# Latent attention heads in eight pairs instead of four groups, in a two-block forward pass in float32

## The chip, the cores and the metric

The kernel runs on one core of a Trainium2 chip. The metric is the device time of one execution in microseconds (us), lower is better; the time quoted is the median of several executions.

## The reference

One sequence of 256 tokens, width 1024, goes through a block of two layers and then through a second block with three further attentions and a mixture of experts. The change touches only the attention of the first block's second layer:

```python
def mla_attention(u, q_lora_norm, w_dq, w_uq, w_o, k_nope, k_rope, v, cos, sin):
    cq = rmsnorm(u @ w_dq, q_lora_norm)                  # 256 tokens x 256
    q = jnp.einsum('bsr,rhd->bshd', cq, w_uq)            # 16 heads x (128 + 64)
    q_nope = q[..., :QK_NOPE_DIM]
    q_rope = apply_rope(q[..., QK_NOPE_DIM:], cos[None, :, None], sin[None, :, None])
    ...
        s = (jnp.einsum('bqhd,bkhd->bhqk', qn_b, k_nope)
             + jnp.einsum('bqhr,bkr->bhqk', qr_b, k_rope))   # per block of 128 queries
        s = s.astype(jnp.float32) * scale
        s = jnp.where(mask[None, None], s, -jnp.inf)         # causal
        p = jax.nn.softmax(s, axis=-1).astype(v.dtype)
        return jnp.einsum('bhqk,bkhd->bqhd', p, v)
    ...
    return o @ w_o                                       # (16 * 128) x 1024
```

K and V of the 16 heads are made from one latent of 128 numbers a token: `k_nope = c_kv @ w_uk`, `v = c_kv @ w_uv`; the rotary key is shared by all heads.

## The kernel before

Every weight passes through a ring of three slots. The SyncE queue (SP) loads a block into `RAW`, of at most 128 x 2048 numbers, as soon as `lo_ready` says that the slot is free. ScalarE (ACT) rounds it to fp32r in `WH` and VectorE (DVE) writes the remainder `RAW - WH` to `WL`; both steps are called `prep`. TensorE (PE) then multiplies in three fp32r passes (`product`: high by high, high by low, low by high) and signals `w_used`. Matmuls on plain float32 data (scores, rotation, outputs) are two passes each in the trace. All orders are written out by hand, one instruction stream for each engine, tied by semaphores.

The latent attention has this order. PE makes the compressed query (`dq`), the keys of the 16 heads (`uk`; ACT copies them to `KN`) and the values (`uv`, eight products of 512 columns, alternately in the PSUM banks `GB` and `UB`; DVE copies them to `V`). Then come four groups of four heads. Group `g` has its query weights in three blocks of the ring. PE makes all queries of the group in `ACC`, ACT copies them to `T`, PE multiplies the rotary part by a rotation matrix into `MB`, and DVE makes the rope in three steps (`rope`: times cosine, the rotated times sine, sum). PE writes the scores of the four heads to the four banks of `ACC`, which is why the next group's queries can start only when the scores have been read. In front of the softmax ACT and DVE prepare the next group's three blocks, or in the last group the first three blocks of the output projection `wo` (`latent_parts`, `blocks`). DVE adds the mask into `PR` and takes the maxima (`group_scores`), ACT makes the exponentials and their sums in place (`group_probs`), and DVE scales them; PE turns the probabilities (`turn`), ACT copies them to `PT`, PE multiplies them with `V` (`weigh`), and ACT and DVE store the output as high and low part in `OH` and `OL` (`group_outputs`). PE begins the next group only when the last output of this one has been stored (`at_ol`). After the fourth group the projection takes eight blocks of 24 matmuls (`down`), and the next feed-forward stage follows. The other attentions of the kernel use the same helpers.

## Time and profile before

| | |
|---|---|
| median of three executions | 2256.55 us (2255.88 to 2256.81) |
| profiled execution | 2257.95 us, its span 2256.2 us |
| busy: PE, DVE, ACT | 2004.4, 1381.1, 996.8 us |
| mean granted TensorE clock | 0.945 of 2.4 GHz |
| values, groups and projection | 691.45 to 849.95 us of the span |

Times within the span are in us from its start. A row of the timeline gives the start, the busy time, the engine, the line, the operation with what it writes and reads, and in brackets how long the engine had stood idle and which instruction released it. The granted clock has two levels here, 1.00 (2.4 GHz) and 0.50 (1.2 GHz); a value between is a mean over a stretch. PEld is PE's weight load, which lies beside its matmuls.

### The profile page before, as it was taken

How to read it: one execution, taken by the hardware profiler on the slowest of the kernel's cores; microseconds unless marked ns; L12 is line 12 of the kernel's file. 1: busy time of each engine (PE TensorE's matmuls, PEld its weight loads, DVE VectorE, ACT ScalarE, POOL GpSimd, SP SyncE). 2: the span in 40 equal slices, each digit the busy share in tenths (PEclk: the TensorE clock that was granted, in tenths of full speed). 3: DMA queues.
4: the chain of work that ended last, by engine and by line, in shares of the span. 5: the costliest groups of instructions: out<-in, count | busy, mean ns of one | idle time of the engine just before them, and what ended most of it. 6: DMA issues, size and time to landing. Idle time of an engine off the chain costs nothing.

```text
span 2256.2 us, 24516 instructions
## 1 busy us (share of the span) xinstructions
PE 2004.4 (89%) x9607; PEld 1649.7 (73%) x9607; DVE 1381.1 (61%) x1878; ACT 996.8 (44%) x1270; POOL 70.2 (3%) x94
## 2 busy tenths in 40 slices
PE   6998899979997789998987899886779999999995
PEld 5787688768876567886766678775668888877774
DVE  4776566666764547676346655548654445478885
ACT  4344334444344434434335434413534434367774
POOL 1000000000000000000000010000000000000000
PEclk9999899989999999998888999978889999999998
DMA  8776367647761246774103586401236657599994
GB/s 285 237 240 226 119 233 244 228 141 239 235 208 32 72 155 204 246 236 160 57 24 131 168 291 207 155 19 57 75 141 225 220 177 235 176 335 364 359 358 160
DMA packets 293803, 432.80 MB, mean 192 GB/s; under 512 B 12164, under 2 KB 244935, under 8 KB 293431
## 3 DMA queue, kind: packets, MB, share of 16 engines
q1 hardware_dynamic: 273696, 356.65, 47.6%
q0 software_dynamic: 17792, 66.99, 8.5%
q10 hardware_dynamic: 2198, 7.58, 0.8%
q8 instruction: 76, 1.25, 0.2%
q14 instruction: 41, 0.33, 0.0%
HBM read 422.27 MB, written 14.68 MB: 194 GB/s over the span
## 4 chain that ended last, share of the span: by engine, by line
PE 73%; issue 10%; DVE 10%; ACT 4%; DMA 1%; ACTq 0%; POOLq 0%; POOL 0%; DVEq 0%; SPq 0%
PE acc L1742 8%; PE acc L1744 8%; PE acc L1743 8%; PE gate_bank L1742 7%; PE gate_bank L1743 7%; PE gate_bank L1744 7%; PE up_bank L1742 6%; PE up_bank L1743 6%; PE up_bank L1744 6%; DVE w_low L1083 3%; PE acc L1880 2%; ACT w_high L663 2%; PE turn_bank L1854 1%; DMA raw<-in_e_ffn_up 1%; PE misc_bank L1902 1%
## 5 line engine op out<-in xcount | busy, mean ns | idle before, releaser
L1083 DVE TENSOR_TENSOR w_low<-raw,w_high 128x2048 fp32r<-128x2048 f32 (+5 forms) x388 | 779.4, 2020 | 506.9 <-ACT w_high L663 506.8
L663 ACT CAST w_high<-raw 128x2048 fp32r<-128x2048 f32 (+5 forms) x388 | 651.8, 1692 | 634.8 <-PE acc L1744 306.5
L1742 PE MATMUL acc<-w_high,hidden_high 128*128 128x512 f32 x682 | 275.2, 404 | 16.5 <-DVE hidden_low L1681 9.4
L1743 PE MATMUL acc<-w_low,hidden_high 128*128 128x512 f32 x682 | 269.2, 395 | 0.0
L1744 PE MATMUL acc<-w_high,hidden_low 128*128 128x512 f32 x682 | 268.3, 393 | 0.0
L1742 PE MATMUL gate_bank<-w_high,u_high 128*128 128x512 f32 (+2 forms) x620 | 246.0, 397 | 19.7 <-DVE w_low L1083 8.6
L1743 PE MATMUL gate_bank<-w_low,u_high 128*128 128x512 f32 (+2 forms) x620 | 238.7, 385 | 0.0
L1744 PE MATMUL gate_bank<-w_high,u_low 128*128 128x512 f32 (+2 forms) x620 | 238.7, 385 | 0.0
L1742 PE MATMUL up_bank<-w_high,u_high 128*128 128x512 f32 (+1 forms) x588 | 228.5, 389 | 0.0
L1744 PE MATMUL up_bank<-w_high,u_low 128*128 128x512 f32 (+1 forms) x588 | 227.7, 387 | 0.0
L1743 PE MATMUL up_bank<-w_low,u_high 128*128 128x512 f32 (+1 forms) x588 | 227.7, 387 | 0.0
L1139 DVE SCALAR_TENSOR_TENSOR ada_sums<-raw_ada,silu_c,ada_sums 128x256 f32<-128x256 f32 x336 | 163.0, 485 | 12.0
L1742 PEld LDWEIGHTS acc<-w_high,hidden_high 128*128 128x128 f32 x682 | 128.2, 188 | 47.3 <-DVE w_low L1083 9.5
L1744 PEld LDWEIGHTS acc<-w_high,hidden_low 128*128 128x128 f32 x682 | 128.0, 188 | 31.9
L1742 PEld LDWEIGHTS gate_bank<-w_high,u_high 128*128 128x128 f32 x620 | 118.6, 191 | 42.5 <-issue 19.1
L1743 PEld LDWEIGHTS acc<-w_low,hidden_high 128*128 128x128 f32 x682 | 128.2, 188 | 27.8
L1744 PEld LDWEIGHTS gate_bank<-w_high,u_low 128*128 128x128 f32 x620 | 118.2, 191 | 23.6
L1743 PEld LDWEIGHTS gate_bank<-w_low,u_high 128*128 128x128 f32 x620 | 118.7, 191 | 20.1
L1744 PEld LDWEIGHTS up_bank<-w_high,u_low 128*128 128x128 f32 x588 | 112.0, 191 | 22.8
L1742 PEld LDWEIGHTS up_bank<-w_high,u_high 128*128 128x128 f32 x588 | 112.0, 190 | 22.6
L1743 PEld LDWEIGHTS up_bank<-w_low,u_high 128*128 128x128 f32 x588 | 111.8, 190 | 22.7
L751 ACT ACTIVATE probs<-probs,softmax_small 128x128 f32<-128x128 f32 x96 | 42.9, 448 | 69.9 <-DVE softmax_small L1221 57.9
(414 smaller groups left out, 2773.9 us busy)
## 6 DMA issues: line engine op xcount, KB each, us to landing
raw<-in_o_exp_gate SPq DMA_DIRECT2D x80, 512.0 KB, 4.8
raw<-in_o_exp_up SPq DMA_DIRECT2D x80, 512.0 KB, 6.1
raw<-in_o_exp_down SPq DMA_DIRECT2D x40, 1024.0 KB, 6.6
raw_ada<-in_e_ada_w POOLq DMA_DIRECT2D x24, 1024.0 KB, 5.5
raw_ada<-in_o_ada_w POOLq DMA_DIRECT2D x24, 1024.0 KB, 5.4
raw<-in_ffn_pre_wg SPq DMA_DIRECT2D x44, 512.0 KB, 5.7
raw<-in_ffn_pre_wu SPq DMA_DIRECT2D x44, 512.0 KB, 6.9
raw<-in_ffn_pre_wd SPq DMA_DIRECT2D x22, 1024.0 KB, 4.9
```

What stands on the lines that cost most here:

```text
L663: ins = nc.scalar.copy(dst(WH[c % RING]), src(RAW[RAW_SLOT[c]]))
L751: ins = nc.scalar.activation(PR[hh][:, k0:k1], PR[hh][:, k0:k1], ACT.Exp, bias=SM[:, hh, t:t + 1], accum_out=SM[:, hh, 2 + t:3 + t])
L1083: ins = nc.vector.tensor_tensor(dst(WL[c % RING]), src(RAW[RAW_SLOT[c]]), dst(WH[c % RING]).bitcast(F32), ALU.subtract)
L1139: ins = nc.vector.scalar_tensor_tensor(ASUM[:, :], w[:, k, :], CS[:, k:k + 1], ASUM[:, :], ALU.mult, ALU.add)
L1742: nc.tensor.matmul(to, sh, mh, start=first, stop=False, **kw)
L1743: nc.tensor.matmul(to, sh, ml, start=False, stop=False, **kw)
L1744: return nc.tensor.matmul(to, sl, mh, start=False, stop=last, **kw)
L1854: mm = nc.tensor.transpose(SB[:, t * w + j * P:t * w + j * P + P], HF[:, t, j * P:(j + 1) * P], ident)
L1880: mm = nc.tensor.matmul(ACC[:, 512 * hh + k0:512 * hh + k1], q, k, start=(j == 0), stop=(j == len(terms) - 1))
L1902: nc.tensor.matmul(bank[:, 0:S], v(0, hh), PT[hh % 2][:, 0:S], start=True, stop=False, skip_group_check=True)
```

## The change

The 16 heads go in eight pairs. The query weights come in eight blocks of 768 columns instead of twelve of 768 and 384. Queries of a pair lie in half of `ACC` (banks 0 and 1, the rotated part with them) and scores of its two heads in the other half, so that both can be under way; `T` and `PR` hold two pairs. PE's order within iteration `p` is: scores of pair `p`, turns of pair `p-1`, queries and rotation of pair `p+1`, outputs of pair `p-1`. ACT and DVE prepare one weight block in each iteration, two ahead: query blocks, and in iterations 6 and 7 the first two of `wo`. The causal mask is added by PE in PSUM: a fp32r matmul of the identity with a 128 x 128 mask block onto the diagonal part of each score tile. Thus DVE takes the maxima and ACT the exponentials straight from PSUM. The first pair's query block is prepared ahead of ACT's copies of the keys and DVE's copies of the values, and its queries and rotation lie between PE's value products. At the end `wo` blocks 0 and 1 lie between the last pair's scores, turns and outputs. The other attentions keep their order; only the values that their semaphores are compared with change (`queried`, `rotated_by`). Below stand SP's loads, then ACT's part, DVE's and PE's; functions that both ACT and DVE have (`latent_prep`, `latent_output`) do each engine's step of the work named.

```diff
+        IDR, LATER = UH[:, 2, 0:P], UH[:, 2, P:2 * P]
...
-            for g in range(HEADS_A // GH):
-                b = STREAM["uq"] + 3 * g
-                load(b, wq[:, 0, g * UQ:(g + 1) * UQ])
-                load(b + 1, wq[:, 1, g * UQ:g * UQ + UQ // 2])
-                load(b + 2, wq[:, 1, g * UQ + UQ // 2:(g + 1) * UQ])
+            for p in range(PAIRS):
+                load(STREAM["uq"] + p, wq[:, :, p * UQ:(p + 1) * UQ])
...
+            nc.scalar.copy(IDR, const("ident"))
+            nc.scalar.copy(LATER, const("causal")[:, 0:P]).then_inc(at_mask, 1)
+            prep(STREAM["uq"], heads_apart(4))
             for k in range(4):
                 act.wait_ge(*((k_full, k + 1) if k < 3 else (w_used, STREAM["uk"] + 1)))
                 nc.scalar.copy(KN[:, 4 * k:4 * k + 4, :],
...
+            def latent_queries(p):
+                act.wait_ge(at_raw, p + 1 if p == 0 else p + 2)
+                nc.scalar.activation(RAW_ROPE, ACC[:, 512:768], ACT.Copy, scale=ident_scale).then_inc(at_q, 1)
+                act.wait_ge(*((at_raw, 2) if p == 0 else (w_used, STREAM["uq"] + p + 1)))
+                nc.scalar.activation(nope_of(p), two(ACC[:, 0:512]), ACT.Copy, scale=ident_scale).then_inc(at_q, 1)
...
+            latent_prep(1)
+            latent_queries(0)
+            for p in range(PAIRS):
+                latent_prep(p + 2)
+                latent_exp(p, 0)
+                if p:
+                    latent_turned(p - 1, 0)
+                latent_exp(p, 1)
+                if p:
+                    latent_turned(p - 1, 1)
+                if p < PAIRS - 1:
+                    latent_queries(p + 1)
+                if p:
+                    latent_output(p - 1, 0)
+                    latent_output(p - 1, 1)
+            prep(b + 2)
+            for hh in range(2):
+                latent_turned(PAIRS - 1, hh)
+            for hh in range(2):
+                latent_output(PAIRS - 1, hh)
             blocks(b + 3, 7)
...
+            prep(STREAM["uq"], heads_apart(4))
...
+            for j in range(8):
+                if j == 6:
+                    latent_rope(0)
+                dve.wait_ge(*((v_full, j + 1) if j < 7 else (w_used, STREAM["uq"] + 1)))
+                nc.vector.tensor_copy(V[:, j // 4, 512 * (j % 4):512 * (j % 4) + 512],
+                                      (GB, UB)[j % 2][:, :]).then_inc(v_out, 1)
+            latent_prep(1)
+            for p in range(PAIRS):
+                latent_prep(p + 2)
+                latent_max(p, 0)
+                latent_max(p, 1)
+                latent_probs(p, 0)
+                latent_probs(p, 1)
+                if p < PAIRS - 1:
+                    latent_rope(p + 1)
+                if p:
+                    latent_output(p - 1, 0)
+                    latent_output(p - 1, 1)
+            prep(b + 2)
...
+            def latent_queries(p):
+                c = STREAM["uq"] + p
+                ready(c)
+                hold(pe, at_q, 2 + 2 * p if p else 0)
+                hold(pe, at_qr, p)
...
+            def latent_scores(p):
+                pe.wait_ge(at_q, 2 + 2 * p + 2)
+                pe.wait_ge(at_qr, p + 1)
+                nope, roped = nope_of(p), roped_of(p)
+                for hh in range(2):
+                    pe.wait_ge(at_exp, head_of(p, hh) - 1)
+                    bank = ACC[:, 1024 + 512 * hh:1536 + 512 * hh]
+                    for t, (k0, k1) in enumerate(Q_TILES):
+                        q, n = slice(t * P, (t + 1) * P), k1 - k0
+                        nc.tensor.matmul(bank[:, k0:k1], nope[:, hh, q], KN[:, 2 * p + hh, 0:n], start=True, stop=False,
+                                         skip_group_check=True)
+                        nc.tensor.matmul(bank[:, k0:k1], roped[:, q], KRZ[:, hh, 0:n], start=False, stop=False,
+                                         skip_group_check=True)
+                        mm = nc.tensor.matmul(bank[:, k1 - P:k1], IDR, LATER, start=False, stop=True, skip_group_check=True)
+                    mm.then_inc(at_score, 1)
...
+                if j == 3:
+                    pe.wait_ge(q_vec, 2)
+                    pe.wait_ge(k_out, 4)
+                    latent_queries(0)
+                elif j == 5:
+                    latent_rotate(0)
+            pe.wait_ge(v_out, 8)
+            pe.wait_ge(at_mask, 1)
+            for p in range(PAIRS):
+                latent_scores(p)
+                if p:
+                    latent_turn(p - 1, 0)
+                    latent_turn(p - 1, 1)
+                if p < PAIRS - 1:
+                    latent_queries(p + 1)
+                    latent_rotate(p + 1)
+                if p:
+                    latent_weigh(p - 1, 0)
+                    latent_weigh(p - 1, 1)
...
+            for hh in range(2):
+                pe.wait_ge(at_exp, head_of(PAIRS - 1, hh) + 1)
+            latent_down(0)
+            latent_turn(PAIRS - 1, 0)
+            latent_turn(PAIRS - 1, 1)
+            latent_down(1)
+            latent_weigh(PAIRS - 1, 0)
+            latent_weigh(PAIRS - 1, 1)
+            for j in range(2, 8):
+                latent_down(j)
```

## Rows read from the trace of the kernel before

**Rows 1.** The page: busy time, share and instructions of each engine.

```profile
PE 2004.4 (89%) x9607; PEld 1649.7 (73%) x9607; DVE 1381.1 (61%) x1878; ACT 996.8 (44%) x1270; POOL 70.2 (3%) x94
```

**Rows 2.** Windows: length, busy time (instructions) by engine, granted clock, DMA share, GB/s.

```profile
702.90:708.80 5.90, 5.90 (x28) 5.90 (x29) 0.00 (x0) 0.00 (x0) 0.00 (x0) 0.50 0.34 126
...
729.28:733.50 4.22, 4.22 (x35) 4.22 (x36) 0.00 (x0) 0.00 (x0) 0.00 (x0) 1.00 0.00 0
733.50:738.10 4.60, 1.45 (x5) 0.41 (x3) 2.10 (x4) 3.32 (x8) 0.00 (x0) 1.00 0.00 0
738.10:743.50 5.40, 5.37 (x32) 4.75 (x32) 5.24 (x15) 1.97 (x8) 0.00 (x0) 1.00 0.54 150
743.50:753.00 9.50, 6.44 (x29) 5.25 (x29) 5.42 (x20) 5.38 (x16) 0.00 (x0) 0.82 0.00 0
...
805.04:850.00 44.96, 44.95 (x192) 35.96 (x192) 17.18 (x8) 13.38 (x7) 0.00 (x0) 1.00 0.44 141
```

**Rows 3.** Timeline from the keys to the first group.

```profile
687.07 1.02 ACT L847 COPY k_nope<-acc 128x1024 f32<-128x1024 f32 x1 [0.24 <-PE acc L1744]
...
693.87 0.68 DVE L1357 COPY v_latent<-gate_bank 128x512 f32<-128x512 f32 x1
...
694.60 0.50 PE L1742 MATMUL gate_bank<-w_high,ckv_high 128*128 128x512 f32 x1 [1.51 <-DVE v_latent L1357]
...
702.89 0.55 PE L1742 MATMUL acc<-u_high,w_high 128*128 128x256 f32 x1 [3.13 <-DVE w_low L1083]
```

**Rows 4.** Timeline of the second group.

```profile
735.25 1.93 ACT L663 CAST w_high<-raw 128x512 fp32r<-128x512 f32 x6
...
737.99 2.09 DVE L1083 TENSOR_TENSOR w_low<-raw,w_high 128x512 fp32r<-128x512 f32 x6
...
738.13 0.49 PE L1880 MATMUL acc<-k_nope,scratch 128*128 128x128 f32 x2 [1.58 <-DVE scratch L1207]
...
740.00 0.55 DVE L1215 TENSOR_TENSOR probs<-acc,consts 128x384 f32<-128x384 f32 x1
...
740.59 0.61 DVE L1221 TENSOR_REDUCE softmax_small<-probs 128x1 f32<-128x128 f32 x2
...
741.23 0.40 ACT L751 ACTIVATE probs<-probs,softmax_small 128x128 f32<-128x128 f32 x1 [4.05 <-DVE softmax_small L1221]
...
745.64 0.55 DVE L1234 TENSOR_SCALAR probs<-probs,softmax_small 128x128 f32<-128x128 f32 x2
...
749.94 0.55 PE L1895 MATMUL up_bank<-consts,probs 128*128 128x128 f32 x3
```

**Rows 5.** Groups by line and shape, 676 to 860 us: count, busy us, mean ns.

```profile
L663 ACT CAST w_high<-raw 128x2048 fp32r<-128x2048 f32 x13 | 24.7, 1917 | 29.7 <-PE acc L1744 28.6 <-PE up_bank L1744 1.1
L751 ACT ACTIVATE probs<-probs,softmax_small 128x256 f32<-128x256 f32 x16 | 7.9, 493 | 0.0
L751 ACT ACTIVATE probs<-probs,softmax_small 128x128 f32<-128x128 f32 x16 | 6.4, 402 | 18.5 <-DVE softmax_small L1221 17.7
...
L763 ACT COPY probs_turned<-gate_bank 128x384 f32<-128x384 f32 x8 | 3.8, 478 | 2.5 <-PE gate_bank L1895 2.5
...
L868 ACT CAST o_high<-misc_bank 128x256 fp32r<-128x256 f32 x8 | 3.0, 372 | 4.3 <-PE misc_bank L1904 4.3
...
L864 ACT ACTIVATE scratch<-acc 128x512 f32<-128x512 f32 x4 | 2.4, 592 | 0.0
...
L1083 DVE TENSOR_TENSOR w_low<-raw,w_high 128x256 fp32r<-128x256 f32 x12 | 4.7, 418 | 0.0
...
L1370 DVE TENSOR_TENSOR o_low<-turn_bank,o_high 128x256 fp32r<-128x256 f32 x8 | 3.4, 424 | 3.9 <-ACT o_high L868 3.9
```

**Rows 6.** Timeline of the last group.

```profile
785.54 6.69 DVE L1083 TENSOR_TENSOR w_low<-raw,w_high 128x2048 fp32r<-128x2048 f32 x3
...
797.39 0.90 PE L1895 MATMUL gate_bank<-consts,probs 128*128 128x128 f32 x3 [6.20 <-DVE probs L1234]
```

**Rows 7.** DMA issues, 660 to 830 us: count, KB each, median us to landing.

```profile
raw<-in_w_o SPq DMA_DIRECT2D x8, 1024.0 KB, 7.0
```

More of the change, by code:

```diff
@@ L1200, in ffn, with rope @@
                     prep(b0 + 3 * count + 1)
-            def rope(g, raw, to, cos, sin, off, bank):
+            def rope(g, raw, to, cos, sin, bank):
                 chain.link(nc.vector.tensor_tensor(to, raw, wide(cos, 2), ALU.mult))
-                dve.wait_ge(at_rot, g + off)
+                dve.wait_ge(at_rot, rotated_by(g))
                 chain.link(nc.vector.tensor_tensor(raw, two(bank), wide(sin, 2), ALU.mult))
@@ new lines, in latent_probs, with latent_output @@
+            def latent_probs(p, hh):
+                h = probs_of(p, hh)
+                dve.wait_ge(at_exp, head_of(p, hh) + 1)
+                chain.link(nc.vector.reciprocal(SM[:, h, 6:8], SM[:, h, 2:4]))
+                for t, (k0, k1) in enumerate(Q_TILES):
+                    ins = nc.vector.tensor_scalar(PR[h][:, k0:k1], PR[h][:, k0:k1], SM[:, h, 6 + t:7 + t], None, ALU.mult)
+                ins.then_inc(at_prob, 1)
+            def latent_output(p, hh):
+                dve.wait_ge(at_oh, head_of(p, hh) + 1)
+                nc.vector.tensor_tensor(OL[:, 2 * p + hh, :], (MB, SB)[hh][:, 0:S], OH[:, 2 * p + hh, :].bitcast(F32),
+                                        ALU.subtract).then_inc(at_ol, 1)
@@ new lines, in latent_rotate @@
+            def latent_rotate(p):
+                pe.wait_ge(at_q, 2 + 2 * p + 1)
+                nc.tensor.matmul(ACC[:, 768:1024], rot, RAW_ROPE, start=True, stop=True).then_inc(at_rot, 1)
+            def latent_scores(p):
+                pe.wait_ge(at_q, 2 + 2 * p + 2)
+                pe.wait_ge(at_qr, p + 1)
+                nope, roped = nope_of(p), roped_of(p)
+                for hh in range(2):
+                    pe.wait_ge(at_exp, head_of(p, hh) - 1)
+                    bank = ACC[:, 1024 + 512 * hh:1536 + 512 * hh]
+                    for t, (k0, k1) in enumerate(Q_TILES):
+                        q, n = slice(t * P, (t + 1) * P), k1 - k0
[5 more added lines that the diff above has]
+                    mm.then_inc(at_score, 1)
@@ new lines, in latent_turn, with latent_weigh @@
+            def latent_turn(p, hh):
+                h = head_of(p, hh)
+                pe.wait_ge(at_prob, h + 1)
+                pe.wait_ge(at_pt, h - 1)
+                for j in range(3):
+                    mm = nc.tensor.transpose((GB, UB)[hh][:, j * P:(j + 1) * P],
+                                             PR[probs_of(p, hh)][:, j * P:(j + 1) * P], ident)
+                mm.then_inc(at_turned, 1)
+            def latent_weigh(p, hh):
+                h = head_of(p, hh)
+                pe.wait_ge(at_pt, h + 1)
+                pe.wait_ge(at_ol, h - 1)
+                bank, at = (MB, SB)[hh], slice((2 * p + hh) * VD, (2 * p + hh + 1) * VD)
+                nc.tensor.matmul(bank[:, 0:S], V[:, 0, at], PT[hh][:, 0:S], start=True, stop=False, skip_group_check=True)
+                nc.tensor.matmul(bank[:, P:S], V[:, 1, at], PT[hh][:, S:], start=False, stop=True,
+                                 skip_group_check=True).then_inc(at_pv, 1)
```

160 lines of the change are left out of this document (75 added, 85 removed).

## The prediction

> **What bounds the kernel now.** I read the page first: over the whole span the tensor engine (PE) is busy 89%, ahead of VectorE (DVE) and ScalarE (ACT) [rows 1]. The change touches only the latent attention, so I cut that stage out with busy time by window, then read its timeline and its chain of waits. The four groups of four heads run from 702.89 us [rows 3] to the first output-projection matmul at 805.04 [rows 2], 102.15 us. A group has four stretches, shown for the second one [rows 2]: 36 query matmuls (4.2 us, PE full); 4.6 us in which PE has 1.45 us of work, because ACT copies the queries out, PE rotates, and DVE makes three rope steps; scores (5.4 us, PE full); 9.5 us of softmax, turning and outputs with PE busy 6.44, part of it at the half clock (granted 0.82). Group two to four PE thus stands or crawls about 9 of 23.7 us. The last group is worse: DVE splits three whole projection blocks in front of the softmax (6.69 us), and PE waits 6.20 us [rows 6]. Two further pauses precede the groups: 1.51 us on a copy of V and 3.13 us on the split of the first query weights [rows 3], after which PE runs 5.9 us at the half clock [rows 2]. So here the end is set by hand-overs, not by PE's work; from 805.04 on PE is full at clock 1.00 [rows 2] and everything behind moves with it.
>
> **What a pair costs each engine.** Kinds and widths are those of today.
> PE: 18 query matmuls at 0.12 (35 in 4.22 us), 2.15. Rotation, one 256-column f32 matmul (two passes), 0.43. Scores: 32 passes for four heads in 5.37 us less the tail of the last [rows 2], so 1.31 a head, 2.62. Turns 0.39 a head (three 128-column transposes: 0.55 less the tail of the last, 0.16) [rows 4], 0.78. Outputs have half the passes of a head's scores, 0.65 a head, 1.3. New: four mask matmuls of 128 columns in one fp32r pass. No row has this form. From below, half a 256-column query matmul, 0.06; from above, a 128-column transpose, 0.13. I take 0.11, nearest to a 128-column f32 pass; 0.44 a pair, both ends 0.24 to 0.52. Sum 7.7 us a pair, 62 for eight.
> ACT: weights' high part, 768 columns: half of the six casts in 1.93 [rows 4], 0.95. Exponentials: per head 0.40 and 0.49 and two accumulator reads, partly overlapped, 0.98, so 1.96. Turned copies 0.96; raw rope queries, 256 columns, 0.38 as the other 256-column copy; nope queries, 512 columns, 0.59; outputs 0.74 [rows 5]. Sum 5.6.
> DVE: low part 1.0 (half of 2.09). Maxima 0.61 a head [rows 4], now read from PSUM. A read from PSUM costs no more by two rows of 256 columns: 0.42 for the outputs' low part, from PSUM, and 0.42 for a weight split, from SBUF [rows 5]. The mask addition of 0.55 a head [rows 4] is gone, 8.8 us over 16 heads, of which only what stood on the chain counts. Normalisation 0.65 a head (two scalings in 0.55 [rows 4] and a reciprocal), rope 3 times 0.42 with 256 columns, outputs 0.85. Sum 5.7.
> The exponentials now read PSUM. Today a 384-column copy from PSUM takes 0.48 and a 256-column exponential from SBUF 0.49 [rows 5], so the bounds are nothing and 0.1 less for each of 32, 3.2 us in all; I take nothing, since the copy has no bias and no sum to keep. The Trainium skill, "VectorE: DVE Perf Modes", section on the TRN2 errata, gives ScalarE 172 cycles fixed from PSUM against 224 from SBUF; an estimate by it at 1.2 GHz is 43 ns less each, 1.4 us in all, 2229.2 for the forecast. No row here isolates it.
>
> **One iteration of the new loop.** Let S be PE's start on scores of pair p. From today's rows: a head's maxima can start 0.46 after its scores are issued (738.13 plus 1.41 to 740.00), and ACT follows DVE within 0.05 [rows 4]. I follow the steady iterations 2 to 5.
> ACT finishes the outputs of the pair before at S+0.6 and casts the next weights until S+1.5. DVE splits them until S+2.55. This is queued in front of the first maximum, which could have begun at S+2.0: the wait that takes the old one's place. Maxima end 3.16 and 3.77. ACT: first exponentials to 4.17, turned copy to 4.65, second to 5.63, turned copy to 6.11, raw queries to 6.53. PE has meanwhile issued scores (to 3.06), turns (3.84) and queries (5.98) and waits 0.6 for the raw copy; rotates 6.6 to 7.0; outputs to 8.3. If ACT is late here, PE's next items, the outputs and then the next scores, are late with it. Rope on DVE ends at 8.07, just under the outputs, so scores of the next pair start at S+8.3. PE has 7.7 of that, so this is near its own bound. Iteration 1 has no late split: 7.8. Iteration 0 has no turns or outputs to cover the rope: 7.2. Iteration 6 splits a 2048-column block (ACT 1.9, DVE 2.23): maxima start at S+4.75, everything shifts 2.2, 10.5. Iteration 7 has the same and no queries, but the projection can start only when the second output is issued: 9.1. Sum 7.2+7.8+4x8.3+10.5+9.1 = 67.8 us.
>
> **The start.** ACT now casts the mask and identity (0.5) and the first query block (0.95) in front of the copies of K; the 0.5 is for two copies of 128 columns, each under the 0.37 of 256 [rows 5]. The first K copy today starts 687.07 [rows 3], just in time for PE to reuse the bank; it will end 1.2 later, and PE with it. DVE splits the first query block (1.0) in front of V. So the first V copy slips by 2.2, from 693.87 to about 696.1 [rows 3], and PE waits 2.8 us where it waited 1.51. Then two V products, queries of pair 0 (2.15), two V products, the rotation 0.43, two more: PE ends about 704.0. DVE's rope (1.26) stands in front of the last two V copies, for which PE waits: S of pair 0 is 705.65.
>
> **The end.** The first projection block could start at 705.65+67.8 = 773.5 instead of 805.04, 31.5 earlier. Two turns and two outputs of the last pair now lie between blocks, 2.1 us of PE. Is the projection fed? One block is 24 matmuls, an eighth of the 192 in 44.9 us, 5.6 us [rows 2]. Block 3 is cast after the last output: 0.8+1.9+2.25 = 4.95 us behind the last weighing, under the 5.6 of block 2. So nothing there, but only 0.7 of cover: each us more is lost. Loads: eight of 384 KB in place of twelve, the same bytes; each buffer is freed three iterations (25 us) before its use. SP's queue is moved past nothing else, POOL's stands still. Gain 29.4.
>
> **The clock.** Three places have PE idle for over 2 us: before the third V product (2.8), in iteration 6 (2.8) and in iteration 7 (3.1). Today an idle of 3.13 was followed by 5.9 us at half clock [rows 2, 3], in which half the work, 2.9 us, is lost. New: V and queries after the first idle, of which V is partly DVE's time, 2.0; after the last ones, the beginning of the projection, 1.5 of at most 2.9. Old half-clock stretches inside the groups were in the measured 102 us already. I take 3.5 us off. The Trainium skill, "TensorE: Matmul & The Clock Gate", Part 1, says that throttled is the default and that activity releases it; the trace agrees, with full clock in each dense stretch. By that rule a denser loop keeps 2.4 GHz, and it would make rival one below more likely.
>
> **Rivals.**
> One: no half clock, and PE's own bound holds in iterations 2 to 5: 3.5 and 4x0.6 less, 2224.7. For it, 93% busy PE; against it, the late split. 0.17.
> Two: the loop's chain is longer. It has ten hand-overs; at 0.1 us more each the period is 9.3: 8 us, 2238.6. For it, today's gaps of ACT behind PE of 0.2 to 0.5; against it, most are counted. 0.18.
> Three: the projection starves. Its loads of 1 MB landed in 7.0 us [rows 7] against 5.6 of use; if they don't overlap, 8x1.4 = 11 us, 2241.8. Against it: DMA share 0.44 in that stretch [rows 2]. 0.05.
> Four, slower: PE stays at the half clock throughout the loop, since its pauses recur every 8 us, at the rotation. Work is then 15.4 a pair, 8x7.1 = 57 more, 2287. It decides from a mean period of 11.6 us on, where 26 us of gain are gone, that is when half of PE's work runs at half clock. For it, granted 0.82 in the softmax stretch [rows 2]; against it, 1.00 in every dense stretch. 0.03.
> Five: nothing comes of it, the stage being held by something unseen, 2256. All pauses have named releasers, so 0.02.
>
> **The numbers.** 29.4 less 3.5 is 25.9. The profiled execution took 2257.95 us with a span of 2256.2; the median of three is 2256.55. The difference applies to each alike, so the span would be 2230.3 and the median 2230.6. The forecast has 0.55, within 2226 to 2236. Range 2223 to 2242: it takes in rivals one to three at their centres and both ends of the mask's price (1.6 less, 0.6 more in eight pairs). A measurement of this kernel can tell about 0.2%, 4.5 us. Faster 0.95, same 0.02, slower 0.03.
>
> **What would show it.** In the changed profile: first scores near 706 us; starts of scores 8.3 us apart; ahead of each, a maximum that follows the weights' split and not the scores; a wait of some 0.6 us at the rotation; iterations 6 and 7 longer by 2 us; no PE gap over 1 us in the projection; its first block near 775.5, its last matmul near 824. Wrong it would be if the period is over 9.5, if mask matmuls take over 0.3 each, or if granted clock in the loop is under 0.9.

## The result and the profile after

The changed kernel takes 2223.15 us (median of four, 2221.89 to 2224.30) against 2256.22 for the kernel before (four, 2254.25 to 2256.81). The ratio is 0.985, with a 95% interval of 0.9838 to 0.9862: 33.1 us, or 1.5%, faster. The forecast was 2230.6, so the direction held and the gain was put 7.5 us too low. The range began at 2223, a ratio of 0.9851 to the 2256.55 that the forecast started from; the measured 0.985 lies on that edge or just beyond it.

The page of the changed kernel begins with busy time, share and instructions of each engine, to be read against [rows 1].

```profile
PE 1993.7 (90%) x9647; PEld 1647.9 (74%) x9647; DVE 1375.4 (62%) x1866; ACT 995.0 (45%) x1272; POOL 70.4 (3%) x94
```

PE has 40 instructions more and is busy 10.7 us less. Where the gain lies is read from windows: length, busy time by engine with instructions, granted clock, DMA share, GB/s. Here is the whole stage, first in the kernel before and then in the changed one.

```profile
685.46:849.49 164.03, 129.78 (x661) 106.81 (x659) 81.43 (x172) 68.73 (x150) 0.00 (x0) 0.93 0.28 93
687.18:818.00 130.82, 120.39 (x701) 105.36 (x699) 75.23 (x160) 65.76 (x152) 0.00 (x0) 0.99 0.35 114
```

PE's busy time fell by 9.4 us although 32 mask matmuls came in, while the mean granted clock rose from 0.93 to 0.99: work that ran at half clock before now runs at full clock. The other 23.8 us are idle time of PE, 34.3 before and 10.4 after. The next windows are all of the changed kernel. The first stretch goes from the first key product to the first scores, the second holds the eight iterations up to the first projection matmul. Then follow iterations 2 to 5, iteration 6, iteration 7, and the projection.

```profile
687.18:706.55 19.37, 14.95 (x98) 12.90 (x96) 9.25 (x19) 10.04 (x22) 0.00 (x0) 1.00 0.11 33
706.55:770.92 64.37, 58.36 (x399) 54.34 (x399) 45.81 (x130) 38.77 (x118) 0.00 (x0) 0.99 0.33 107
721.20:751.90 30.70, 30.70 (x218) 29.15 (x217) 22.59 (x69) 19.70 (x64) 0.00 (x0) 1.00 0.35 117
751.90:761.83 9.93, 7.87 (x57) 7.31 (x55) 6.83 (x17) 5.79 (x15) 0.00 (x0) 1.00 0.31 106
761.83:770.92 9.09, 6.25 (x37) 5.28 (x35) 5.99 (x14) 5.01 (x13) 0.00 (x0) 0.90 0.32 115
773.00:819.00 46.00, 46.00 (x206) 37.03 (x204) 20.57 (x12) 15.73 (x13) 0.00 (x0) 1.00 0.50 162
```

In iterations 2 to 5 PE is busy for the whole 30.70 us at clock 1.00; a group of the kernel before left it idle for 6.2 of 23.7 us and gave it a mean clock of 0.82 in the last 9.50 [rows 2]. The projection is full as before. What is left idle is in the chain of waits of PE over the stage: who waited for whom, us in total, times, longest.

```profile
PE misc_bank L2142 <- ACT probs_turned L899: 2.7, 1, 2.7
PE gate_bank L1834 <- DVE v_latent L1458: 2.4, 1, 2.4
PE acc L2110 <- ACT scratch L883: 2.1, 1, 2.1
PE acc L2121 <- DVE v_latent L1458: 1.4, 1, 1.4
PE acc L2121 <- ACT scratch L885: 1.1, 1, 1.1
...
PE acc L1834 <- ACT k_nope L873: 0.6, 1, 0.6
```

Three of the six are at the start (keys, values), one follows iteration 0, one is in iteration 6 at the rotation, one in iteration 7.

**How the stage is measured below.** PE's work ahead of the first key product is the same in all kernels here, yet that product started between 684.9 and 689.2 us in their profiled executions, and what lies behind the stage took 1400.2 to 1406.7 us. Whole-kernel times therefore scatter by a few us for reasons outside the stage. So each kernel also gets a stage time, from its first key product to the start of the second pass of the last product of the output projection: 164.03 us before (685.46 to 849.49) and 130.82 after (687.18 to 818.00), 33.2 us less, which is the whole gain of the medians. A stage time comes from one execution, so it also holds what the clock did in that one. Stage marks agreed between kernels to about 0.1 us wherever their code is the same. One execution of the first sequential kernel below, at granted clock 0.82, is left out of every comparison.

| kernel | stage | to first scores | iterations 2 to 5, each | iteration 6 | iteration 7 | ratio to before (interval) |
|---|---|---|---|---|---|---|
| changed | 130.82 | 19.37 | 7.68 | 9.92 | 9.09 | 0.985 (0.9838 to 0.9862) |
| e_same_iteration | 133.59 | 19.41 | 8.12 | 10.31 | 10.6 | 0.9856 (0.984 to 0.9872) |
| e_sequential_2 | 159.85 | 19.38 | 11.4, 12.8 in turn | 13.53 | 9.14 | 0.9974 (0.9958 to 0.9989), by e_sequential |
| a_no_mask | 131.25 | 19.39 | 7.67 | 11.38 | 9.18 | 0.9845 (0.9828 to 0.9861) |
| a_mask_dve | 139.55 | 19.37 | 8.08 to 8.68 | 12.17 | 9.82 | 0.9875 (0.9859 to 0.9891) |
| b_prep_late | 125.63 | 19.37 | 7.59 | 8.39 | 6.48 | 0.9825 (0.9812 to 0.9839) |
| b_prep_late_no_mask | 123.25 | 19.39 | 7.19 | 8.39 | 6.48 | 0.9827 (0.9812 to 0.9842) |
| c_start_undone | 134.58 | 21.75 | 7.67 | 11.53 | 9.12 | 0.9873 (0.9858 to 0.9888) |
| d_tail_undone | 132.44 | 19.36 | 7.67 | 9.91 | 13.4 | 0.9851 (0.9836 to 0.9867) |
| f_start_only | 130.68 | 16.86 | 7.67 | 11.17 | 9.12 | 0.9847 (0.983 to 0.9865) |
| g_start_and_prep | 124.00 | 16.84 | 7.59 | 8.4 | 6.47 | 0.9831 (0.9817 to 0.9845) |

Experiments 1 to 10 below are, in this order, e_sequential_2, e_same_iteration, a_no_mask, a_mask_dve, b_prep_late, b_prep_late_no_mask, c_start_undone, d_tail_undone, f_start_only and g_start_and_prep. Times are in us. Iteration 7 counts up to the first projection matmul. In e_same_iteration, e_sequential_2 and d_tail_undone it therefore holds the last pair's turns and outputs too, which elsewhere lie between projection blocks.

### The profile page after: what moved, and what is told of

It is laid out like the page before. It is cut to its first block, busy times and chain, and to the rows that moved or that the text cites. A ratio compares the mean times of both kernels' runs of the same rounds, so it can differ in the third digit from the quotient of the medians.

```text
span 2220.6 us, 24598 instructions
## 1 busy us (share of the span) xinstructions
PE 1993.7 (90%) x9647; PEld 1647.9 (74%) x9647; DVE 1375.4 (62%) x1866; ACT 995.0 (45%) x1272; POOL 70.4 (3%) x94
## 3 DMA queue, kind: packets, MB, share of 16 engines
q8 instruction: 76, 1.25, 0.2%
## 4 chain that ended last, share of the span: by engine, by line
PE 73%; issue 10%; DVE 9%; ACT 5%; DMA 1%; ACTq 0%; POOLq 0%; POOL 0%; DVEq 0%; SPq 0%
PE acc L1834 8%; PE acc L1835 8%; PE acc L1836 8%; PE gate_bank L1834 7%; PE gate_bank L1836 7%; PE gate_bank L1835 7%; PE up_bank L1834 6%; PE up_bank L1836 6%; PE up_bank L1835 6%; DVE w_low L1140 3%; ACT w_high L686 2%; PE acc L1972 1%; PE turn_bank L1946 1%; DMA raw<-in_e_ffn_up 1%; ACT normed_rows L692 1%
## 5 line engine op out<-in xcount | busy, mean ns | idle before, releaser
L1140 DVE TENSOR_TENSOR w_low<-raw,w_high 128x2048 fp32r<-128x2048 f32 (+2 forms) x380 | 779.5, 2060 | 499.6 <-ACT w_high L686 499.3
L686 ACT CAST w_high<-raw 128x2048 fp32r<-128x2048 f32 (+2 forms) x380 | 652.0, 1725 | 616.4 <-PE acc L1836 291.9
L1834 PE MATMUL acc<-w_high,hidden_high 128*128 128x512 f32 x682 | 275.7, 404 | 16.5 <-DVE hidden_low L1773 9.4
L1834 PE MATMUL gate_bank<-u_high,w_high 128*128 128x256 f32 x168 | 54.6, 325 | 17.7 <-DVE u_low L1172 8.3
```

What stands on the lines that cost most here:

```text
L686: ins = nc.scalar.copy(dst(WH[c % RING]), src(RAW[RAW_SLOT[c]]))
L1140: ins = nc.vector.tensor_tensor(dst(WL[c % RING]), src(RAW[RAW_SLOT[c]]), dst(WH[c % RING]).bitcast(F32), ALU.subtract)
L1834: nc.tensor.matmul(to, sh, mh, start=first, stop=False, **kw)
```

## Experiments

All edits are to the changed kernel. Orders are changed on PE, ACT and DVE together; where only PE's part is shown, the other two follow it.

**1. Is it the order? Pairs one after the other.** Eight pairs, mask in PSUM and interleaved start stay; queries of the next pair go behind the outputs of this one.

```diff
             for p in range(PAIRS):
                 latent_scores(p)
-                if p:
-                    latent_turn(p - 1, 0)
-                    latent_turn(p - 1, 1)
+                latent_turn(p, 0)
+                latent_turn(p, 1)
+                latent_weigh(p, 0)
+                latent_weigh(p, 1)
                 if p < PAIRS - 1:
                     latent_queries(p + 1)
                     latent_rotate(p + 1)
-                if p:
-                    latent_weigh(p - 1, 0)
-                    latent_weigh(p - 1, 1)
...
-            latent_down(0)
-            latent_turn(PAIRS - 1, 0)
-            latent_turn(PAIRS - 1, 1)
-            latent_down(1)
-            latent_weigh(PAIRS - 1, 0)
-            latent_weigh(PAIRS - 1, 1)
-            for j in range(2, 8):
+            for j in range(8):
                 latent_down(j)
```

> The changed kernel with its pairs one after another: PE does scores, turns and outputs of a pair, and only then queries and rotation of the next; ACT and DVE in the same order; the projection's first two blocks no longer lie between the last pair's steps. Mask in PSUM, pairs, the start among the V products stay. Theory A (the order within the loop is the gain): per pair PE waits for maxima, exponentials, scaling and turned copies (about 3 us) and for the raw copy and the rope (about 1.5), so starts of scores are 11 to 12 us apart instead of 7.68: 24 to 30 us over seven pairs, time 2248 to 2254, most of the gain gone. Rival B (the mask off DVE and the earlier start are the gain): less than 10 us lost, under 2234.

The same kernel was profiled a second time, for its rows:

> A second look at the pairs one after another, for its rows: starts of scores 11 to 12 us apart by theory A, under 9 by rival B, granted clock in the loop under 1.00 where PE waits.

The median was 2253.27 us, ratio 0.9974 (0.9958 to 0.9989), and the second profile's execution took 2251.57. The stage takes 159.85 us, 29.0 more than in the changed kernel, and the starts of scores lie 11.4 and 12.8 us apart in turn. Its eight iterations as a window, and then the waits of PE in them:

```profile
708.39:803.91 95.52, 71.38 (x413) 61.09 (x413) 47.30 (x132) 43.03 (x122) 0.00 (x0) 0.92 0.22 72
```

```profile
PE gate_bank L2123 <- DVE probs L1427: 12.8, 8, 2.3
PE acc L2111 <- ACT scratch L885: 7.6, 7, 1.1
PE up_bank L2123 <- DVE probs L1427: 3.7, 8, 0.5
```

Each pair waits for its own softmax before both turns (16.5 us in all) and for its own queries before its scores (7.6). PE also takes 71.38 us for 413 matmuls where the changed kernel takes 58.36 for 399, at clock 0.92 against 0.99; the 14 more are the last pair's turns and outputs. Over the whole stage both have 701 matmuls: 18.1 of the 29.0 us are idle time of PE and 10.9 busy time (131.33 for 120.39, at clock 0.95 for 0.99). So the order, in the loop and at its end, is worth 29.0 of the 33.2 us, by waits and by clock together; the end alone is 1.6 (experiment 8). Smaller pairs, the PSUM mask and the interleaved start bring the other 4.2 between them when the order is missing; they were not taken apart in that form.

**2. How far apart must the pieces be?** Queries of the next pair still lie between scores and softmax, but turns and outputs of a pair stay in its own iteration. The projection's blocks all follow the last outputs, as in experiment 8.

```diff
             for p in range(PAIRS):
                 latent_scores(p)
-                if p:
-                    latent_turn(p - 1, 0)
-                    latent_turn(p - 1, 1)
                 if p < PAIRS - 1:
                     latent_queries(p + 1)
                     latent_rotate(p + 1)
-                if p:
-                    latent_weigh(p - 1, 0)
-                    latent_weigh(p - 1, 1)
+                latent_turn(p, 0)
+                latent_turn(p, 1)
+                latent_weigh(p, 0)
+                latent_weigh(p, 1)
```

> The changed kernel with each pair's turns and outputs in its own iteration: PE does scores of a pair, queries and rotation of the next, then turns and outputs of the same pair; the projection's blocks all behind them. Theory A1 (queries between scores and softmax are most of it, the outputs one iteration later add little): the 2.6 us of queries and rotation nearly cover maxima, exponentials and scaling, period 8.1 to 8.6 us instead of 7.68, so 3 to 7 us lost in the loop and 1 to 3 at its end, 2227 to 2233. Rival A2 (both are needed, since each leaves PE waiting for ACT): period 9.5 or more, 2238 or more.

The median was 2223.14 us, no measurable difference from the changed kernel and less than the 2227 to 2233 expected. The stage was 2.8 us longer, where 4 to 10 were expected, with a period of 8.12, inside the expected 8.1 to 8.6. PE's waits:

```profile
PE gate_bank L2123 <- DVE probs L1427: 3.8, 1, 3.8
...
PE misc_bank L2132 <- ACT probs_turned L899: 1.7, 7, 0.2
```

The 2.6 us of queries and rotation cover nearly the whole softmax of a pair: only 0.24 us an iteration is left at the turned copies, and 3.8 once at the end. Queries between scores and softmax carry nearly all of the gain; moving the outputs an iteration later adds 2.8 us at most, of which the undone end alone makes 1.6 (experiment 8).

**3. What do the mask matmuls cost?** The mask is left out altogether; nothing else changes.

```diff
-                        nc.tensor.matmul(bank[:, k0:k1], roped[:, q], KRZ[:, hh, 0:n], start=False, stop=False,
-                                         skip_group_check=True)
-                        mm = nc.tensor.matmul(bank[:, k1 - P:k1], IDR, LATER, start=False, stop=True, skip_group_check=True)
+                        mm = nc.tensor.matmul(bank[:, k0:k1], roped[:, q], KRZ[:, hh, 0:n], start=False, stop=True,
+                                              skip_group_check=True)
```

> The changed kernel without the four mask matmuls of a pair and without any causal mask in this attention (that part of the computation is left out). 32 matmuls less, which took about 0.12 to 0.13 us each. Theory P (in the steady loop PE's work is the bound): 0.5 us less in each of eight pairs, period 7.2, 3.5 to 4 us faster than the changed kernel, about 2219.3. Theory C (ACT's and DVE's chain from the outputs over the weights' split, maxima, exponentials to the rotation has no slack either): its last step ended 0.07 us before PE was free in the changed kernel, so the period stays 7.5 to 7.65 and PE waits for the raw copy instead: 0.5 to 1.5 us faster, 2222.

The median was 2222.44 us, and the period stays 7.67 us. The time that PE saves comes back as a wait at the rotation, in the timeline of iteration 3 (start, busy time, instruction, idle time before it and its releaser):

```profile
733.44 0.43 ACT L883 ACTIVATE scratch<-acc 128x256 f32<-128x256 f32 x1
...
733.92 0.48 PE L2110 MATMUL acc<-scratch,consts 128*128 128x256 f32 x1 [0.21 <-ACT scratch L883]
```

The matmul before the rotation starts at 733.43, so the rotation starts 0.49 behind it, where the changed kernel has 0.12 (726.94 to 727.06): the whole saving is back as waiting. So the bound of these iterations is 7.67, the chain of weights' split, maxima, exponentials, raw queries on DVE and ACT, and PE's own work of 7.59 (experiment 5) lies within 0.1 of it. PE reads 100% busy, and still a cheaper PE brings nothing here. Iterations 0 and 1 do become 0.4 shorter each, 6.63 and 7.23. The stage is even 0.4 longer, because iteration 6 took 11.38 here (see the clock below).

**4. The mask on DVE.** The old form within the new order: DVE adds the mask into `PR`, maxima and exponentials read `PR`.

```diff
+                chain.link(nc.vector.tensor_tensor(pr[:, :], bank[:, 0:P + S], const("causal"), ALU.add))
...
-                    ins = nc.vector.tensor_reduce(SM[:, probs_of(p, hh), t:t + 1], bank[:, k0:k1], AX_X, ALU.max, negate=True)
+                    ins = nc.vector.tensor_reduce(SM[:, probs_of(p, hh), t:t + 1], pr[:, k0:k1], AX_X, ALU.max, negate=True)
```

> The changed kernel with the mask where it was: DVE adds it into the probabilities' buffer, maxima and exponentials read that buffer, and PE has no mask matmuls. DVE has 0.55 more a head, both on the chain that leads to the raw copy and the rope. Theory C: the chain is longer by 0.6 to 1.1 a pair while PE has 0.5 less, period 8.2 to 8.7, 4 to 8 us slower than the changed kernel, 2227 to 2231. Theory P (PE bound, DVE with slack): the mask's move cost PE 0.5 a pair and gave nothing, so this is 3 to 4 us faster than the changed kernel, about 2219.5.

The median was 2230.08 us, the stage 8.7 longer. The timeline of one iteration shows the addition in the chain, and the rotation's wait at its end:

```profile
749.02 0.55 DVE L1426 TENSOR_TENSOR probs<-acc,consts 128x384 f32<-128x384 f32 x1
749.60 0.61 DVE L1428 TENSOR_REDUCE softmax_small<-probs 128x1 f32<-128x128 f32 x2
...
750.25 0.40 ACT L891 ACTIVATE probs<-probs,softmax_small 128x128 f32<-128x128 f32 x1 [2.21 <-DVE softmax_small L1428]
...
750.65 0.50 ACT L891 ACTIVATE probs<-probs,softmax_small 128x256 f32<-128x256 f32 x1
...
753.19 0.70 PE L2112 MATMUL acc<-scratch,consts 128*128 128x256 f32 x2 [0.93 <-ACT scratch L883]
```

The mask in PSUM takes 0.55 us a head from the engine that stands in the chain, for 0.40 us a pair on PE (experiment 6). In iterations 2 to 5 that is worth 0.4 to 1.0 us each, 2.8 in all. But the 8.7 us of the stage are not the chain alone. Here are iterations 1, 6 and 7 and the 6 us behind them:

```profile
712.18:721.50 9.32, 9.15 (x50) 8.28 (x51) 5.74 (x18) 3.89 (x13) 0.00 (x0) 0.82 0.17 42
755.03:767.20 12.17, 9.00 (x53) 8.01 (x51) 8.23 (x19) 5.91 (x15) 0.00 (x0) 0.86 0.23 86
767.20:777.02 9.82, 6.01 (x32) 5.16 (x31) 6.67 (x15) 5.14 (x13) 0.00 (x0) 0.84 0.32 107
777.02:783.00 5.98, 5.98 (x21) 4.75 (x21) 2.72 (x2) 2.17 (x2) 0.00 (x0) 0.70 0.03 7
```

By these clocks 6.7 us were lost at half clock, against 1.6 in the changed kernel (see below), so some 5 of the 8.7 us are the clock. How much of that the longer waits caused is not shown.

**5. The weights' preparation off the chain.** ACT and DVE prepare a block behind the pair's softmax instead of in front of its maxima, and DVE's low parts of the outputs move behind the first maximum of the next iteration.

```diff
             latent_prep(1)
+            latent_prep(2)
             for p in range(PAIRS):
-                latent_prep(p + 2)
                 latent_max(p, 0)
+                if p > 1:
+                    latent_output(p - 2, 0)
+                    latent_output(p - 2, 1)
                 latent_max(p, 1)
                 latent_probs(p, 0)
                 latent_probs(p, 1)
                 if p < PAIRS - 1:
                     latent_rope(p + 1)
-                if p:
-                    latent_output(p - 1, 0)
-                    latent_output(p - 1, 1)
+                    latent_prep(p + 3)
+            for hh in range(2):
+                latent_output(PAIRS - 2, hh)
```

> The changed kernel with the weights' preparation moved off the chain: ACT casts the block of iteration p+3 behind the copies of the next queries and in front of the outputs, DVE splits it behind the rope, and DVE takes the low part of the outputs one iteration later, between the two maxima. Nothing is left out. Theory C: in the steady iterations PE's own work (7.68) bounds as well, so the period stays 7.65 to 7.7; in iterations 6 and 7, where the projection's 2048-column blocks are prepared (PE waited 2.06 and 2.74 us), the first maximum comes 1 to 1.5 us earlier: 2 to 3 us faster than the changed kernel in the stage, 2220 to 2221.5. Rival P2 (the waits in iterations 6 and 7 come from the exponentials and turned copies themselves): no change of those waits.

The median was 2217.62 us (five runs, 2214.18 to 2221.36), the stage 5.2 us shorter, about twice the expectation. Steady iterations, iteration 6 and iteration 7 as windows:

```profile
723.19:753.55 30.36, 30.36 (x219) 28.91 (x217) 21.75 (x68) 19.72 (x63) 0.00 (x0) 1.00 0.37 118
753.55:761.94 8.39, 7.84 (x56) 7.28 (x55) 6.54 (x16) 6.05 (x16) 0.00 (x0) 1.00 0.34 125
761.94:768.42 6.48, 5.46 (x37) 4.72 (x35) 5.67 (x14) 3.68 (x14) 0.00 (x0) 1.00 0.41 126
```

And the first maximum of an iteration, in the timeline of DVE:

```profile
738.29 1.03 DVE L1141 TENSOR_TENSOR w_low<-raw,w_high 128x512 fp32r<-128x512 f32 x2
...
740.09 0.62 DVE L1427 TENSOR_REDUCE softmax_small<-acc 128x1 f32<-128x128 f32 x2 [0.77 <-PE acc L2129]
```

The maximum now waits for the scores, and DVE stands 0.77 us in front of it: the late split that the prediction named as the new wait is gone. Only 0.09 of each steady iteration hung on it, since PE needs 7.59 alone; the 2048-column blocks of iterations 6 and 7 made the rest: 1.53 and 2.61. The projection is 0.7 shorter too. With the waits there cut to 0.55 and 0.75 the clock also stays at 1.00 in iteration 7 and behind it, where it was 0.90 and 0.87; that is 1.6 of the 5.2 us.

**6. The same without the mask**, the edits of 3 and 5 together.

> The same, and without mask matmuls and any causal mask in this attention (that part is left out). This with the run before it is the test of what the chain through the weights' preparation held. Theory C: with that chain shortened the missing 0.5 us of PE's work now shows, the period falls to 7.15 to 7.3, 2.5 to 3.5 us faster over the loop than with the mask. Rival: another chain (weighing, outputs, rope) holds at 7.6: no gain from it, as it was with the preparation in its old place, where the period stayed at 7.67.

The median was 2216.31 us, with a period of 7.19, inside the expected 7.15 to 7.3. Now that DVE and ACT have slack, the four mask matmuls show their price: 0.40 us an iteration, 0.10 each.

**7. The start undone.** Query block 0 is prepared behind the keys and values, and its queries and rotation come behind all value products.

```diff
-                if j == 3:
-                    pe.wait_ge(q_vec, 2)
-                    pe.wait_ge(k_out, 4)
-                    latent_queries(0)
-                elif j == 5:
-                    latent_rotate(0)
+            pe.wait_ge(q_vec, 2)
+            pe.wait_ge(k_out, 4)
+            latent_queries(0)
+            latent_rotate(0)
```

> The changed kernel with the start as before the change: the first query block is prepared behind ACT's copies of the keys and DVE's copies of the values, and the first pair's queries and rotation follow all eight value products. From the first key product to the first scores the changed kernel takes 19.4 us; here PE waits 1.5 at the third value product and about 2 on the first block's split (one block of 768 columns, where the kernel before had three), then 2.6 us of queries and rotation, copies and rope 1.3 uncovered: 22.5 to 25, so 3 to 5.5 us slower than the changed kernel, 2226 to 2229, of which up to 3 come from the half clock if it falls after the wait. Rival (the start gives nothing, since the same waits return elsewhere): within 1 us.

The median was 2228.35 us, the stage 3.8 longer: 2.4 before the first scores and 1.6 in iteration 6, which has the same waits as in the changed kernel but a clock of 0.85 for 1.00. The first scores come after 21.75 us, sooner than the expected 22.5 to 25. Here is that stretch:

```profile
686.96:708.71 21.75, 17.02 (x99) 13.72 (x97) 9.74 (x19) 10.29 (x22) 0.00 (x0) 0.92 0.12 36
```

PE's waits in it add up to 4.6 us, against 4.4 in the changed kernel. What grew is PE's busy time, 17.02 for 14.95, with a clock of 0.92 for 1.00, which is a loss of 1.7. So most of the 2.4 us is the clock, and the move of the first pair's queries is worth less than 1 us beside it. All four executions (2227.31 to 2229.05) were slower than all of the changed kernel's, so the loss itself is clear; whether the clock falls there each time is not shown.

**8. The tail undone.** The projection's blocks 0 and 1 come behind the last pair's outputs.

```diff
-            latent_down(0)
             latent_turn(PAIRS - 1, 0)
             latent_turn(PAIRS - 1, 1)
-            latent_down(1)
             latent_weigh(PAIRS - 1, 0)
             latent_weigh(PAIRS - 1, 1)
-            for j in range(2, 8):
+            for j in range(8):
                 latent_down(j)
```

> The changed kernel with the last pair's turns and outputs in front of the whole projection instead of between its first blocks. Worked out from the changed kernel's rows: PE waits about 1 us for the turned copies and the projection starts 2.5 to 3.5 us later, but the 2.1 us of turns and outputs no longer lie inside it: 0.5 to 1.5 us slower over the stage. Rival (the interleaving hides the whole softmax of the last pair, as the two first blocks' 11 us would suggest): 4 us or more slower.

The median was 2224.74 us, the stage 1.6 longer, just over the expected 0.5 to 1.5. The last outputs wait once more for their turned copies:

```profile
773.00 0.70 PE L2142 MATMUL misc_bank<-probs_turned,v_latent 128*128 128x256 f32 x2 [1.36 <-ACT probs_turned L899]
```

**9. An earlier start.** Block 0 is prepared behind the key copies on ACT and between value copies on DVE; the split of block 2 goes behind the first softmax, and the first scores no longer wait for all value copies.

```diff
             for j in range(8):
+                if j == 2:
+                    latent_prep(0)
                 if j == 6:
                     latent_rope(0)
...
-            pe.wait_ge(v_out, 8)
             pe.wait_ge(at_mask, 1)
             for p in range(PAIRS):
                 latent_scores(p)
+                if p == 1:
+                    pe.wait_ge(v_out, 8)
```

> The changed kernel with a shorter start, nothing left out: ACT casts the first query block behind its copies of the keys and of the compressed query, DVE splits it between the second and the third value copy, the first scores no longer wait for the last two value copies (the first turns do), and in iteration 0 DVE splits the third block behind the scalings. Chain theory: the wait at the third value product falls from 2.44 to about 1.4, the key stall of 0.58 and the 1.41 in front of the first scores go, and the first maxima come up to 1 us later behind the value copies: 1.5 to 2.8 us faster from the first key product to the last of the projection. Rival: the first scores start earlier, but iteration 0 is longer by as much, since DVE has the same work in front of the first maximum: under 0.7 us.

The first scores come 2.5 us sooner (16.86), but the stage is only 0.1 shorter and the median was 2224.73. Iteration 0 takes 0.9 more, as the first maxima still stand behind the last value copies and a weights' split on DVE, and iteration 6 takes 1.25 more, at a clock of 0.88 where the changed kernel had 1.00. So the rival's number (under 0.7) came, but only half for its reason: without the half clock 1.4 would have been left. The windows of iteration 6 and of one us in it:

```profile
749.74:760.91 11.17, 9.11 (x57) 8.29 (x55) 7.19 (x17) 5.78 (x15) 0.00 (x0) 0.88 0.26 94
759.00:760.00 1.00, 1.00 (x4) 0.88 (x4) 0.51 (x2) 0.13 (x1) 0.00 (x0) 0.50 0.00 0
```

**10. Both, 5 and 9.**

> Both versions that should be faster in one kernel, nothing left out: the shorter start and the preparation off the chain. They touch different iterations (0 and the start; 6 and 7), so by the chain theory the gains add: 3.5 to 5.5 us in the stage against the changed kernel, 2218 to 2220. Rival: the start's gain is taken back in the steady loop.

The stage takes 124.00 us, 6.8 less than in the changed kernel (3.5 to 5.5 were expected; 1.6 is the changed kernel's half clock) and 1.6 less than in 5. The median was 2218.41 us (2216.83 to 2222.17), ratio 0.9831 (0.9817 to 0.9845), which cannot be told from 5. By the stage both beat the changed kernel. By the whole time 5 is 5.5 us under it, with intervals that just touch, and 10 is 4.7 under, with intervals that overlap.

## Why the prediction put the gain too low

**What held.** The stage was set by hand-overs, and the order takes them out (experiment 1). Rival one came close, with 0.17: PE is full in the steady loop, and of the 3.5 us of half clock that it takes away 1.6 were there. Rivals two to five did not come. Neither a longer chain, nor a starved projection (busy 46.00 of 46.00), nor a half clock through the loop is in the trace. The first maximum does follow the weights' split. Here is iteration 2, which starts at S = 721.20:

```profile
721.67 0.93 ACT L686 CAST w_high<-raw 128x512 fp32r<-128x512 f32 x2
...
722.63 1.03 DVE L1140 TENSOR_TENSOR w_low<-raw,w_high 128x512 fp32r<-128x512 f32 x2 [0.40 <-ACT w_high L686]
...
723.58 0.62 DVE L1426 TENSOR_REDUCE softmax_small<-acc 128x1 f32<-128x128 f32 x2
...
724.23 0.37 ACT L891 ACTIVATE probs<-acc,softmax_small 128x128 f32<-128x128 f32 x1 [1.63 <-DVE softmax_small L1426]
...
724.59 0.47 ACT L891 ACTIVATE probs<-acc,softmax_small 128x256 f32<-128x256 f32 x1
...
725.03 0.48 ACT L899 COPY probs_turned<-gate_bank 128x384 f32<-128x384 f32 x1
...
725.39 0.39 ACT L891 ACTIVATE probs<-acc,softmax_small 128x128 f32<-128x128 f32 x1
...
726.20 0.50 ACT L899 COPY probs_turned<-up_bank 128x384 f32<-128x384 f32 x1
...
726.56 0.43 ACT L883 ACTIVATE scratch<-acc 128x256 f32<-128x256 f32 x1
...
727.06 0.68 PE L2110 MATMUL acc<-scratch,consts 128*128 128x256 f32 x2
```

The maximum starts at S+2.38 for a forecast of S+2.55. PE's cost of a pair, forecast as 7.7, is 7.59 where nothing else holds it (experiment 5), and a mask matmul is 0.10 for 0.11. Reading scores from PSUM costs the maxima nothing (0.62, against 0.61).

**The step that failed: the loop's chain on ACT.** The prediction gave an iteration 8.3 us, with PE waiting 0.6 at the rotation. It is 7.68, without a wait. The raw queries were to be copied at S+6.53; the row above ends at 726.99, S+5.79. The prediction added up ACT's busy times. But starts lie closer than these: the 384-column copy is busy 0.48 and the next instruction starts 0.36 after it (725.03 to 725.39), and the two exponentials of a head take 0.80 from their first start to the next copy (724.23 to 725.03), where 0.98 was put down. For two heads and two copies that is 2 x 0.18 + 2 x 0.12 = 0.6 us an iteration, just the forecast wait; the rest of the 0.74 is the maximum that starts 0.17 earlier. The Trainium skill, "ScalarE: Activation LUTs", section "What ACT_TABLE_LOAD costs", says that back-to-back ACTIVATEs overlap by about 93 ns; the trace shows 0.11 to 0.12 here, and the sum had left it out for the copies.

**What each term cost.** The forecast stage was 164.03 less 25.9, 138.13; measured 130.82, so 7.3 us are to be found.

| term | forecast | measured | difference |
|---|---|---|---|
| iterations 2 to 5 | 4 x 8.3 | 30.71 | 2.5 |
| iterations 0, 1 | 7.2 and 7.8 | 7.03 and 7.62 | 0.35 |
| iteration 6 | 10.5 | 9.92 | 0.6 |
| iteration 7 | 9.1 | 9.09 | 0.0 |
| first key product to first scores (705.65 less 685.46) | 20.19 | 19.37 | 0.8 |
| half clock at the start | 2.0 | none | 2.0 |
| projection, with what lies between its blocks and its half clock | 48.05 | 47.08 | 1.0 |

The sum is 7.25. The rest is rounding: 805.04 less 773.45 is 31.59, put down as 31.5. Two slips of the prediction change nothing in it: DVE's terms of a pair add up to 5.6, not 5.7, and PE "stands or crawls" in a group of the kernel before for 6.2 us of idle time and 1.7 lost at half clock [rows 2], not for 9. The start was late by the slip of the first value copy, which came out as a wait of 2.44 us for a forecast of 2.8. This is the second failed term: after the 3.13 us pause of the kernel before, PE ran 5.9 us at half clock [rows 2, 3], and the prediction took a 2.8 us pause to do the same. After the 2.44 the whole stretch to the first scores has clock 1.00. At the other end it did fall, after the wait of 2.74 in iteration 7:

```profile
768.43 0.70 PE L2142 MATMUL misc_bank<-probs_turned,v_latent 128*128 128x256 f32 x2 [2.74 <-ACT probs_turned L899]
...
769.61 1.22 PE L2142 MATMUL turn_bank<-probs_turned,v_latent 128*128 128x256 f32 x2
```

The same two passes take 0.60 in iteration 2. The clock was 0.90 over the 9.09 us of iteration 7, a loss of 0.10 x 9.09 = 0.9 us. From 770.92 to 776.60 it was 0.87, another 0.7. Together 1.6, for 1.5 forecast at this end, against 3.5 for both places, and half of it lies in front of the projection's first matmul and not behind it. That iteration 7 came out as forecast is therefore luck: at full clock it would have taken 8.2, not 9.1.

**The exponentials from PSUM.** They take 0.37 and 0.47 first in a pair, 0.39 and 0.49 second; with the mask on DVE, reading SBUF, 0.40 and 0.50. So 0.01 to 0.03 less each, within the bounds of nothing and 0.1. The 43 ns by the page "VectorE: DVE Perf Modes" of the Trainium skill, cited in the prediction, was more than any of these rows show.

**Where the rest of the gain could have been.** The prediction costed iterations 6 and 7 at 2 us over the others and left it at that. Experiment 5 shows that these, and not the steady loop, are what the place of the preparation decides: 4.1 of its 5.2 us.

## What to carry to other kernels

Where a pair's work is a ring of hand-overs, put the next pair's independent matmuls between its scores and its softmax; that one move carried nearly all of the gain, and the rest of the interleaving added little. For a chain on one engine add the distances between starts, not the busy times. When PE reads 100% busy, still check whether another chain ends at the same moment: in the steady iterations here, leaving out PE's mask matmuls alone gave nothing, moving the weights' split off the chain alone gave 0.09 us each, and both together 0.49. Read the granted clock in every window before a difference is put down to an edit: 1.7 us came and went with it several times here.

## What the runs showed of the hardware

The granted clock answered the same wait differently. Iteration 6 has the same matmuls and the same wait of PE at the rotation in the changed kernel (2.06 us), in experiment 8 (2.05), in experiment 7 (2.06) and in experiment 9 (2.06); it takes 9.92, 9.91, 11.53 and 11.17 us. In experiment 3 the wait is 2.46 and the iteration takes 11.38. The window of experiment 3, beside the ones above at 1.00 and 0.88:

```profile
751.11:762.49 11.38, 8.92 (x52) 7.97 (x51) 7.14 (x17) 5.78 (x15) 0.00 (x0) 0.85 0.27 92
```

At full clock this iteration is 1.2 to 1.6 us cheaper. The wait of 2.44 us at the start lowered the clock in none of the eight kernels that have it (1.00 up to the first scores in each); in experiment 7 the clock fell in that stretch, behind a wait of 1.81. The wait of 2.74 in iteration 7 of the changed kernel was followed by half clock. The Trainium skill, "TensorE: Matmul & The Clock Gate", Part 1, says that the activity monitor runs free of the kernel, so that the point of a transition varies from run to run. The rows agree with that, but do not isolate it. What decides it in a given execution stays open, and so does whether the changed kernel's other executions had the favourable case. In experiments 5, 6 and 10, with no wait over 1.2 us in iterations 6 and 7, the loop's clock was 1.00. But short waits were no guarantee: in experiment 4 the clock fell to half at the start of iteration 1 (0.82 over it), behind waits of 0.44 and 1.12 us, while iteration 1 of the changed kernel, behind one of 1.11, had 1.00.
